# Experts of a mixture layer on one core: weights as the moving operand, 64 tokens stationary, matmuls on the two halves of the array's columns

## The reference

```python
D_MODEL, N_EXPERTS, TOP_K, D_EXPERT = 1024, 32, 2, 512
def hier_moe(h, ...):                       # h: rmsnorm of the tokens
    g_prob = softmax(hf @ w_router_group + b);  g_idx, g_w = argmax(g_prob), max(g_prob)
    e_prob = softmax(e_logits of group g_idx);  top_v, top_i = top_k(e_prob, TOP_K)
    weights = g_w[:, None] * top_v / sum(top_v)
    expert = g_idx[:, None] * EXPERTS_PER_GROUP + top_i
    ...                                     # rows sorted by expert, padded to blocks
    def expert_block(xb, e):
        return (silu(xb @ w_gate[e]) * (xb @ w_up[e])) @ w_down[e]
    y = sum over a token's two rows of out * weight
x = x + hier_moe(rmsnorm(x, norm_ffn), ...)
```

## Time and profile before

| what | value |
|---|---|
| median of 3 runs | 2503.28 us (2489.35 to 2503.91) |
| span of the profiled execution | 2502.2 us |
| TensorE busy | 2137.1 us (85%) |
| VectorE, GpSimd, ScalarE busy | 865.1, 609.5, 568.6 us |
| DMA | 374.40 MB, mean 150 GB/s |
| mean granted TensorE clock | 0.880 |

### The profile page before, as it was taken

The page is one execution under the profiler, slowest core; times in us unless marked ns, Lnnn a source line. Parts: engine busy times, 40 slices in busy tenths (PEclk is TensorE's granted clock), DMA queues, the critical chain, the costliest instruction groups (busy, mean ns, idle before and its releaser), DMA issues. The chain is left out here.

```text
span 2502.2 us, 30438 instructions
## 1 busy us (share of the span) xinstructions
PE 2137.1 (85%) x11922; PEld 1710.9 (68%) x11922; DVE 865.1 (35%) x1158; ACT 568.6 (23%) x963; POOL 609.5 (24%) x358
## 2 busy tenths in 40 slices
PE   4877686885889999898899799892999999999993
PEld 3756474763678878776677687441888777788871
DVE  3779697896421222266222222113000000000002
ACT  3223233231231332175443421010000000000000
POOL 4266563738542432211000022001000000000002
PEclk7988788896899999999555699995999999999996
DMA  2412233213222221111850021316788888888875
GB/s 103 113 29 82 67 89 88 64 44 104 84 84 71 81 67 54 56 42 39 246 149 1 26 59 50 113 49 234 283 337 317 315 315 318 323 339 323 316 307 207
DMA packets 231874, 374.40 MB, mean 150 GB/s; under 512 B 8640, under 2 KB 188224, under 8 KB 223488
## 3 DMA queue, kind: packets, MB, share of 16 engines
q1 hardware_dynamic: 224336, 346.40, 40.2%
q0 software_dynamic: 7040, 25.17, 2.6%
q10 hardware_dynamic: 432, 1.96, 0.2%
HBM read 315.89 MB, written 56.03 MB: 149 GB/s over the span
## 5 line engine op out<-in xcount | busy, mean ns | idle before, releaser
L164 PE MATMUL bank<-h_high,w_w_high 128*128 128x256 f32 x960 | 343.0, 357 | 34.1 <-issue 7.7
L164 PE MATMUL bank<-h_low,w_w_high 128*128 128x256 f32 x960 | 333.1, 347 | 0.0
L164 PE MATMUL bank<-h_high,w_w_low 128*128 128x256 f32 x960 | 331.8, 346 | 0.0
L451 POOL TENSOR_TENSOR w_w_low<-w_raw,w_w_high 128x1024 fp32r<-128x1024 f32 x76 | 192.3, 2532 | 480.5 <-ACT w_w_high L446 480.5
L1906 PEld LDWEIGHTS bank<-e_xT,e_wg 128*128 128x128 f32 x2048 | 236.3, 194 | 16.5 <-issue 15.1
L1906 PE MATMUL bank<-e_xT,e_wg 128*128 128x96 f32 x2048 | 235.8, 277 | 1.1 <-DVE e_xT L1927 1.1
L164 PEld LDWEIGHTS bank<-h_high,w_w_high 128*128 128x128 f32 x960 | 193.1, 201 | 63.1 <-issue 38.3
L1906 PE MATMUL bank<-e_xT,e_wu 128*128 128x96 f32 x2048 | 233.9, 275 | 0.0
L1906 PEld LDWEIGHTS bank<-e_xT,e_wu 128*128 128x128 f32 x2048 | 232.2, 193 | 0.0
L1918 PE MATMUL bank<-e_wd,e_act 128*96 128x512 f32 x512 | 225.1, 593 | 1.3 <-ACT e_y L1951 1.3
L794 DVE SCALAR_TENSOR_TENSOR ssd_xc<-ssd_conv_in,ssd_conv_p,ssd_xc 128x774 f32<-128x774 f32 x144 | 202.9, 1409 | 10.8
(11 more groups left out here) (252 smaller groups left out, 3211.1 us busy)
## 6 DMA issues: line engine op xcount, KB each, us to landing
e_wg<-in_w_gate SPq DMA_DIRECT2D x32, 2048.0 KB, 13.4
e_wu<-in_w_up SPq DMA_DIRECT2D x32, 2048.0 KB, 18.1
e_wd<-in_w_down SPq DMA_DIRECT2D x32, 2048.0 KB, 9.4
w_raw<-in_w_in SPq DMA_DIRECT2D x60, 512.0 KB, 4.5
ssd_decays<-decay_sums SPq DMA_DIRECT2D x48, 512.0 KB, 5.8
rows_in<-zeros SPq DMA_DIRECT2D x4, 4512.0 KB, 44.5
e_x<-rows_in SPq DMA_DIRECT2D x32, 384.0 KB, 18.5
rows_out<-e_y POOLq DMA_DIRECT2D x32, 384.0 KB, 7.3
```

Of the source, the lines that this page charges most:

```text
L164: last = pe.matmul(out, lhs[k][a], rhs[k][b], start=(k == 0 and m == 0), stop=(k == n - 1 and m == 2))
L451: pool.tensor_tensor(self.pair[u].low[:, :, :], self.raw[u][:, :, :], self.pair[u].high[:, :, :].bitcast(F32), ALU.subtract).then_inc(self ...
```

## The change

`CAP` becomes 64 and `NBLK` with it 12. There can now be 23 overflow blocks, in 24 places (`NBI` = 24, 56 × 64 rows in `rows_in`).

The hidden part holds 64 tokens stationary and lets 512 columns of weights move, 256 of gate and 256 of up, and there are two such matmuls for each k: one for the first half of the features into partitions 0 to 63 of the PSUM bank, one for the second half into partitions 64 to 127. In the built program they are placed on the two halves of the array's columns (128 rows x 64 columns each). Down is built in the same way from two halves of the output columns. Since the hidden result now has tokens on the partitions, two transposes of the product follow (`pe_act_transpose`, L1908) with a copy by VectorE (`dve_act_T`). Rows are loaded and transposed for two experts at once (128 rows, one buffer). Gate and up share a buffer `e_w` and a semaphore. The stage `overflow_blocks` goes; the loop over overflow blocks stands at the end of `experts`, with its double buffers, and SP takes the block's expert from `core.overflow`. GpSimd stores a block in two halves of 512 columns.

```diff
-CAP = 96
+CAP = 64
...
-NBI = 16
+NBI = 24
...
+        def load_hidden(sp, n, e, u, first=False):
             if not first:
-                sp.wait_ge(gate_mm, e - 1)
-            sp.dma_start(wg[u][:, :, :], core.expert_rows("w_gate", e, KD)).then_inc(wg_in[u], 16)
+                sp.wait_ge(hid_mm, n - 1)
+            for part, name in enumerate(("w_gate", "w_up")):
+                sp.dma_start(w[u][:, part, :, :], core.expert_rows(name, e, KD)).then_inc(w_in[u], 16)
+
+        def load_down(sp, n, e, u, first=False):
             if not first:
...
+                sp.wait_ge(down_mm, n - 1)
+            sp.dma_start(wd[u][:, :, :], core.expert_cols("w_down", e)).then_inc(wd_in[u], 16)
...
+        def pe_hidden(pe, n, u, i, first=False):
+
+            pe.wait_ge(xt_ok, i + 1)
             if not first:
...
+                pe.wait_ge(act_ok, n - 1)
+            pe.wait_ge(w_in[u], 32 * i + 32)
+            for k in range(KD):
+                for half in range(2):
+                    last = pe.matmul(core.bank[2 + u][half * CAP:(half + 1) * CAP, :],
+                                     xT[:, k, u * CAP:(u + 1) * CAP], w[u][:, :, k, half * HALF:(half + 1) * HALF],
+                                     start=(k == 0), stop=(k == KD - 1))
+            last.then_inc(hid_mm, 1)
+
+        def pe_act_transpose(pe, n, u, first=False):
+            pe.wait_ge(act_ok, n + 1)
             if not first:
+                pe.wait_ge(actT_ok, n - 1)
             for j in range(2):
...
+                last = pe.transpose(core.bank[4 + u][:, j * P:(j + 1) * P], act[u][:, j * P:(j + 1) * P], core.ident)
+            last.then_inc(actT_mm, 1)
+
+        def pe_down(pe, n, u, i, first=False):
+            pe.wait_ge(wd_in[u], 16 * i + 16)
+            pe.wait_ge(actT_ok, n + 1)
             if not first:
...
+                pe.wait_ge(y_ok, n - 1)
+            for k in range(KE):
+                for half in range(2):
+                    last = pe.matmul(core.bank[6 + u][half * CAP:(half + 1) * CAP, :], act_T[u][:, k % 2, k // 2, :],
+                                     wd[u][:, k, half * 512:(half + 1) * 512], start=(k == 0), stop=(k == KE - 1))
+            last.then_inc(down_mm, 1)
...
+        def overflow(eng, body):
+
+            there = eng.value_load(core.overflow[0:1, NBI:NBI + 1], min_val=0, max_val=NOV)
+            with eng.If(there > 0):
+                with eng.Fori(0, (NOV + 1) // 2) as j:
+                    for u in range(2):
+                        with eng.If(there > 2 * j + u):
+                            body(NEXP + 2 * j + u, 2 * j + u, u, MAIN + j)
...
                 def pair(i, first=False, last=False):
...
+                    pe_hidden(pe, 2 * i, 0, i, first=first)
+                    if not first:
+                        pe_down(pe, 2 * i - 1, 1, i - 1)
+                    pe_act_transpose(pe, 2 * i, 0, first=first)
+                    pe_hidden(pe, 2 * i + 1, 1, i, first=first)
+                    if not last:
+                        pe_transpose(pe, i + 1)
+                    pe_down(pe, 2 * i, 0, i, first=first)
+                    pe_act_transpose(pe, 2 * i + 1, 1, first=first)
```

More of the change, by code:

```diff
@@ L1852, in experts @@
     own, sb, sem = open_stage(core)
+    HALF = DE // 2
+    MAIN = NEXP // 2
     with own:
[L1854 to L1859, removed]
@@ L1868, in load_rows @@
-        def load_rows(sp, e, u):
-            sp.dma_start(x[u][:, :], core.rows_in[bass.ds(e * CAP, CAP), :]).then_inc(x_in[u], 16)
-        def load(sp, e, u, first=False, last=False):
+        w, wd = (list(pair) for pair in zip(core.first_weights, expert_weights(lambda *args: sb(*args), "e1")))
+        x, xT = sb("e_x", [P, D]), sb("e_xT", [P, KD, P])
+        silu = [sb(f"e_silu{u}", [P, HALF]) for u in range(2)]
+        act = [sb(f"e_act{u}", [P, HALF]) for u in range(2)]
+        act_T = [sb(f"e_actT{u}", [P, 2, 2, CAP]) for u in range(2)]
@@ new lines, in dve_xt, with dve_act @@
+        def dve_xt(dve, i):
+            dve.wait_ge(tr_mm, i + 1)
+            for j in range(2):
+                last = dve.tensor_copy(xT[:, 4 * j:4 * j + 4, :], core.bank[j][:, :].rearrange("p (k r) -> p k r", k=4))
+            last.then_inc(xt_ok, 1)
+        def dve_act(dve, n, u, first=False):
+            dve.wait_ge(silu_ok, n + 1)
+            if not first:
+                dve.wait_ge(actT_mm, n - 1)
+            dve.tensor_tensor(act[u][:, :], silu[u][:, :], core.bank[2 + u][:, HALF:2 * HALF], ALU.mult)\
+                .then_inc(act_ok, 1)
@@ new lines, in _, with body @@
+                pe_act_transpose(pe, 3, 1)
+                with pe.Fori(2, MAIN - 1) as i:
+                    pair(i)
+                pair(MAIN - 1, last=True)
+                pe_down(pe, NEXP - 1, 1, MAIN - 1)
+                def body(n, b, u, i):
+                    if u == 0:
+                        pe_transpose(pe, i)
+                    pe_hidden(pe, n, u, i)
+                    pe_act_transpose(pe, n, u)
+                    pe_down(pe, n, u, i)
+                overflow(pe, body)
@@ L2007, in _, with one @@
-                pair(LAST, last=True)
-            @block.scalar
-            def _(act):
-                def pair(i, first=False):
-                    for u in range(2):
-                        e = 2 * i + u
-                        act_silu(act, e, u, first=first)
-                        if not (first and u == 0):
-                            act_y(act, e - 1, 1 - u, i - (1 - u))
-                pair(0, first=True)
-                with act.Fori(1, NEXP // 2) as i:
-                    pair(i)
-                act_y(act, NEXP - 1, 1, LAST)
+                def one(n, u, first=False):
+                    dve_act(dve, n, u, first=first)
+                    dve_act_T(dve, n, u, first=first)
```

303 lines of the change are left out of this document (104 added, 199 removed).

## The result

The changed kernel takes 2382.95 us (median of 4 runs, 2380.9 to 2384.81), the kernel before 2496.32 us in the same comparison (4 runs, 2488.61 to 2503.91). The ratio is 0.953, with a 95% interval of 0.9492 to 0.9567. The profiled execution took 2384.32 us, its span is 2382.6 us. So the time came out where it was forecast, 2382. The gain is a little under the 121 us forecast: 113 between the two medians, 119.6 between the two profiled spans. The forecast was counted from 2503.3, while the four runs of the kernel before lie in two pairs, 2488.61 and 2489.35, 2503.28 and 2503.91. An agreement within 1 us is therefore in part luck, and the intermediate values decide whether the reasons given were the right ones.

A forecast was written before the change was run, and what follows sets the result against it. TensorE was taken to bound the expert stage before, DMA after. The first gather 122 us earlier, less 1 us outside the stage, gave 2503.3 - 121 = 2382 us; range 2338 to 2465, at 0.82.

The forecast's parts named there:

- TensorE bounds before, and DMA after: Expert stage: TensorE needs 22.0 us an expert before; DMA then becomes the bound at about 17 or 18 us.
- A pair costs one matmul: Hidden and down: two column halves overlap fully, 0.86 us a pair, so 6.9 us for hidden and 3.45 for down.
- TensorE's block is 11.7 us: Expert stage: hidden 6.9, down 3.45 and 1.3 us for transposes and drains make 11.7 us, against 22.0.
- Two overflow blocks, 228.3 MB at 400 GB/s, last transfer at 2318: Expert stage's transfers, two overflow blocks included: 571 us, so the last `wd` lands at 2318.
- DMA remains the bound, by a thin margin.: SP's load order: 11.7 us until more is queued, 14.5 with clock loss, against 17 us of transfers already there.
- The clock costs 2.75 us a block and nothing of the time: TensorE after idling: 5.5 us at half speed lose 2.75 us, 11.7 becomes 14.5, still under the limit.
- The last hidden part starts when its `w` lands, at 2313: Stage's tail: last hidden part begins 5.2 us before `wd` lands and takes 9.6 us; last copy ends at 2329.
- Ten us for empty rounds: Overflow loop after its last block: 22 untaken Ifs and 12 rounds add 10 us, bounds 0 and 20.
- the pairs do not overlap: Rival, hidden and down: column halves run one after the other, 22.0 us a block, +55, 2559 us; chance 0.06.
- the third rival: Expert stage: TensorE and DMA take turns, 18.5 to 20 us a block, 2430 to 2480 us; chance 0.09.
- The clock stays at the lower level: Rival, expert stage: overlapping pairs at half speed take 22.6 us a block, +76, 2579 us; chance 0.06.
- the slower transfers: Rival, expert stage: DMA that never rests gets 358 GB/s, 638 us in place of 571, 2449 us; chance 0.07.

The follow-up runs named there:

- the kernel without `up` loads: The changed kernel with `w_up` loaded for experts 0 and 1 alone and `w_gate` loaded in two pieces: 2279.57 us, ratio 0.9109.
- Down twice: The changed kernel with each down part computed twice, adding TensorE work but no transfers: 2414.48 us, ratio 0.9645.
- `w` first: The changed kernel with SP issuing `w` of block n + 1 ahead of `wd` of block n: 2355.76 us, ratio 0.9426.
- after: The changed kernel itself, without any follow-up edit, against the kernel before: 2382.95 us, ratio 0.953.
- halves in turn: The changed kernel with all matmuls of one column half, then all of the other, in hidden and down: 2448.18 us, ratio 0.9782.
- order by twos: The changed kernel with two matmuls on one column half, then two on the other, in hidden and down: 2381.84 us, ratio 0.9531.
- the kernel with 64 moving columns: The kernel before with only 64 of each expert's 96 rows moving past the weights in gate and up: 2522.97 us, ratio 1.0085.

## Why the prediction was right, step by step

**TensorE bounds before, and DMA after.** Right. The gain is 123 us of stage, forecast as 122, and with 31% less to transfer another 103 us go.

**A pair costs one matmul.** Right: 7.09 us for hidden against 6.9, 3.65 for down against 3.45. Most of the difference is the 0.16 us by which a last record outlasts its place. The nearest row, the two row halves of attention, was the right one to go by. By an estimate from the 2.38 times that the Trainium skill's page "TensorE: Matmul & The Clock Gate", Part 3 (Packing small matmuls), gives for three column tiles, a pair would have cost 1.26 matmuls; the trace has 7.09 / 6.9, or 1.03.

**TensorE's block is 11.7 us.** Right: blocks without a wait in the kernel without `up` loads follow each other after 10.8 us where there are no row transposes, and these add 1.1 us in every second block, so 11.4.

**Two overflow blocks, 228.3 MB at 400 GB/s, last transfer at 2318.** Right in each part. The DMA issues on the profile's page have `e_wd` 34 times, and the windows up to 2325 add up to 219.09 + 9.33 = 228.4 MB. The rate over 400 us is 400 GB/s. Transfers end near 2322.5, in a stretch that began at 1749.55: 573 us, and 572.3 forecast.

**"DMA remains the bound, by a thin margin."** The step that was right in time and incomplete in reason. The margin was there as worked out: the issue at 2017.75 came 4.7 us before the last queued load landed, by its 19.6 us. But it was taken as a switch, full rate as long as anything is queued. Down twice alone does not refute that: with the figures now measured the margin is 17.0 - 11.4 - 1.4 us, less 1 to 2 for issue and first bytes, so 2.2 to 3.2, and of 3.45 us more some would show in any case (0.93 us a block did). `w` first does refute it. It adds and removes no work and takes 0.9 us off each block, and the rate behind each issue of `wd` is 302 GB/s for 2 us in after and 399 there. So the rate of 400, taken from rows of a kernel with the same order of loads, was the right one for this order and not a limit of DMA. The upper bound of 425 GB/s held the 422 of the other order.

**The clock costs 2.75 us a block and nothing of the time.** Right in the tail, half as large elsewhere. Hidden parts took 8.5 us in the mean (288.2 us for 34), so 1.4 us of loss, up to 2.9; the one on the path, of the last block but one, took 10.02, 2.9 more than at full clock. That the loss in the other blocks costs nothing is not shown: if it passes through as the added down part did, 0.93 in 3.45, it is an estimated 0.4 us a block, some 13 in all.

**The last hidden part starts when its `w` lands, at 2313.** This step failed, with no effect on the sum. TensorE did not wait before its last hidden part. It had waited for the one before, until 2303.67, since `x1` lay ahead of those weights, and the two blocks then followed in series, 29 us to the end of the copy at 2332.79. From the first load that is 583.2 us; forecast were 583.3, from 1745.69 to 2329. That two different ways through the last blocks come to the same is luck.

**Ten us for empty rounds.** Right in kind, 7.3 measured; from the copy to the first gather 18.0 us against 19.5.

**The rivals.** The mechanism of "the pairs do not overlap" was priced too high: with the halves in turn it gave 2448 and not 2559, since the array still overlaps four records at each change of half. What its kernel shows is the third rival: blocks of 18.7 us with both engines waiting in turn, priced at 2430 to 2480. "The clock stays at the lower level" fell, as the clock was 0.88 in the stage; so did the slower transfers, with 400 to 422 GB/s.

## What to carry to other kernels

When loads are issued in one order by one engine, order them by when their buffers come free; a load that waits for a later step holds back one that could already go. Here the share over 400 us was 0.99 with the gap and 1.01 without it, while the rate (400 and 422 GB/s) and the time to landing told them apart. If matmuls fill only half of the array's columns, let neighbours in the stream use different halves; here the second half cost 3% as long as no more than two matmuls in a row lay on one half. To find out whether a margin is real, add the work that it is said to hide: here 3.5 us in each block cost 31.5 us with one order of loads and 4.4 with the other.

## What the runs showed of the hardware

- Matmuls on the two column halves overlap across other records in the stream: order by twos is as fast as by ones (7.11 against 7.09 us), and with all of one half first, four records overlap at each change (12.26 us against 13.98), those of the next part in another bank too.
- One core sustained 422 GB/s over 400 us with each `w` issued ahead of the `wd` whose buffer comes free later, and 400 GB/s at a share of 0.99 with the two the other way round. A share near 1 over a long window did not mean a full rate.
- At the stage's start the granted clock was 0.50 for 57 us of uninterrupted records in the kernel with 64 moving columns, and rose in the first down part; in the kernel before it rose within the first gate part, of 10.07 us. Each is one profiled execution.
- 22 untaken Ifs and their loop rounds cost 7.3 us.
- Stages of the same code before the expert stage ended as much as 19 us apart in the profiled executions (1734.59 to 1753.48), which is more than some of the effects looked for; the length of the stage in question is the better measure of them, and it too has a spread of some 5 us.
